# Branch rows split four to a step instead of two, and the branch projections dealt out from two steps sooner

## The chip, the cores and the metric

The kernel runs on one NeuronCore of a Trainium2 chip. The metric is the device time of one launch, in microseconds (us), as the median of several runs. TensorE (PE) does the matrix products; VectorE (DVE), ScalarE (ACT) and GpSimd (POOL) work on rows; SyncE (SP) issues most of the DMA transfers. Each engine takes its own instructions in program order and waits on semaphores for the others, so an instruction that waits holds up everything behind it on its engine.

## The reference, cut to what matters

One layer of a hybrid decoder for 1024 prompt tokens and 32 sample tokens. After a joint input projection three branches run (a state-space scan, dilated attention, attention into a memory); each is projected, gated, and the sum goes through an output projection.

```
h = RMSNorm(x);  u = h @ w_in
y_ssd = RMSNorm(ssd_scan(...) * silu(z))          # 16 heads x 64, chunks of 128 tokens
y_att = dilated_attention(...) * silu(z_att)
y_mem = memory_attention(...) * silu(z_mem)
merged = g0*(y_ssd @ w_br_ssd) + g1*(y_att @ w_br_att) + g2*(y_mem @ w_br_mem)
y = RMSNorm(x + merged @ w_out)
```

## The kernel before

**Precision by splitting.** A product in fp32 is made of three matmuls on a high part (fp32r) and a remainder: high x high, high x remainder, remainder x high (L2268 to L2270). So every operand is split first: ScalarE copies the value into the high part, VectorE subtracts that from the value and writes the remainder. For the weights that is L1363 and L1701, once for each chunk of 256 columns ("split" and "low" in the plan). A chunk's weights are loaded into one shared buffer, and its split is done two chunks ahead.

**Branch rows.** The attention and memory outputs lie in memory transposed, as eight rows of 128 partitions x 1056 tokens, 528 KB each: rows 0 to 3 of attention, 4 to 7 of memory. Before the branch projections each row is loaded by SyncE (L1110, "yal" in the plan) into one of three buffers in turn (yraw, acc1, acc0), copied by ScalarE into the high part (L1595) and subtracted by VectorE (L2094); the last two are "ya" in the plan. The load of row k waits until the remainder of row k-3 is made, since it takes that buffer. The eight rows of the scan's output are treated likewise ("yb": L1130, L1602, L2098), later.

**The scan.** The prompt runs in eight tiles of 128 tokens, here tiles 0 to 7 (tile 6 is the seventh), the sample tokens as a tile 8. The steps of tile c:

- step 0: TensorE transposes the tile (L2651 to L2656), ScalarE copies it out of PSUM (L1613 to L1616), VectorE weights it (L2150 to L2160). SyncE loads the tile (L1148), but only when the readout of the tile before is done.
- steps 1 and 2: decay matrices, two groups of four heads each: TensorE broadcasts (L2667), ScalarE takes a relu (L1628) and an exp (L1632), VectorE masks (L2167).
- step 3: products within the tile (L2687), then the readout of the state (L2695), which writes the PSUM banks 3 and 4. Before it, "step 6" of the tile before: TensorE transposes that tile's normed rows into the same banks (L2705), ScalarE copies them out (L1643) and GpSimd stores them (L1318). The readout waits for that copy, and the transposes wait for the relus of all four groups of the current tile.
- step 4: the tile's output and the new state on VectorE (L2188 to L2214); the second half of the state on TensorE (L2679) waits for VectorE's first half.
- step 5: square, root and norm of the output rows (L1635, L1637, L2219 to L2224).

**Order.** A function, plan(), writes one list of steps by hand; every engine walks through that list and issues its part of each step. Up to tile 6 step 0 the scan is mixed with the last input projections; entries 31 to 34 of the list "core" (tile 6, steps 1 to 4) carry the branch rows; the entries behind them are mixed, by the function spread(), with the branch projections ("p1"): 48 pieces of 12 matmuls (128 x 352, four rows deep), in four chunks (52 to 55) of two output tiles, three thirds of the tokens, and two branches. VectorE multiplies each piece by a gate (L2115, or L2117 and L2119 for the second branch); SyncE loads the gates (L1026, "p1g"), and GpSimd stores each finished output tile (L1290). A piece needs one of three PSUM banks, so TensorE runs at most three pieces ahead of VectorE. The first piece waits for all eight branch rows. Behind p1 come the projection of the scan's output ("p2", chunks 56 to 59, which wait for all eight yb rows) and the output projection.

The plan puts "low" of a chunk behind the next step 3 of a tile if that is within 15 places of its "split", and else directly behind the split.

Of the kernel before, what the change touches and what calls it, by code (L numbers as in the profile page):

```python
# [122 lines left out]
def plan():  # L123
# [73 lines left out]
    def spread(groups, steps):  # L197

        out, done = [], 0
        for i, g in enumerate(groups):  # L200
            out += g
            upto = len(steps) * (i + 1) // len(groups)
            for step in steps[done:upto]:
                out += step
            done = upto
        return out
# [54 lines left out]
    def gate_steps(k):  # L261

        steps = []
        for n in take(k):
            steps += [[s] for s in project(n) + [("split", n)]]
        return steps
# [26 lines left out]
    core = []  # L293
# [7 lines left out]
    core += [[(q, b)] for b in range(BS) for q in ("ssd_sb", "ssd_sd", "ssd_so")]  # L301
    core += [[("ssd_st",)], [("ssd_sy",)]]
    core += [[("ssd", NB, q)] for q in (4, 5, 6)] + [[], []] + [[("yb", k)] for k in range(KT8)]
    n_gate, n_ya = 31, 4
    core[n_gate - 3] += [("yal", k) for k in range(3)]
    for i in range(n_ya):
        core[n_gate + i] += [("yal", k) for k in ((3, 4), (5, 6), (7,), ())[i]]
        core[n_gate + i] += [("ya", 2 * i), ("ya", 2 * i + 1)]
    sched += spread(core[:n_gate], gate_steps(len(fill_src)))
    for x in core[n_gate:n_gate + n_ya]:  # L310
        sched += x
# [18 lines left out]
    for s in [s for s in sched if s[0] == "silu" and s[2] == 1]:  # L330
        i = sched.index(s)
        sched.insert(i + 3, sched.pop(i))
    for s in [s for s in sched if s[0] == "split" and ("low", s[1]) not in sched]:
        i = sched.index(s)
# [5 lines left out]

def build_program(nc, io, outs):
    chunks, sched, units, sets, values, part_end = plan()
    n_chunks = len(chunks)
    order = {}
# [2425 lines left out]
```

## Time and profile before

| | |
|---|---|
| median of 3 runs | 2211.18 us (2209.74 to 2226.33) |
| profiled execution, its own time | 2218.64 us |
| its span, first to last instruction | 2216.9 us |
| mean granted clock of TensorE | 0.959 of full |
| TensorE busy | 2048.2 us, 92% of the span |
| VectorE, ScalarE, GpSimd busy | 1056.7, 804.3 and 237.7 us |

The profile is of one execution, whose time lies 7.5 us above the median. The stretch that the change touches runs from about 1775 us (tile 6, step 1) to 1997 us (the first p2 piece), a tenth of the span.

### The profile page before, as it was taken

How to read it: one execution, taken by the hardware profiler on the slowest of the kernel's cores; microseconds unless marked ns; L12 is line 12 of the kernel's file. 1: busy time of each engine (PE TensorE's matmuls, PEld its weight loads, DVE VectorE, ACT ScalarE, POOL GpSimd, SP SyncE). 2: the span in 40 equal slices, each digit the busy share in tenths (PEclk: the TensorE clock that was granted, in tenths of full speed). 3: DMA queues.
4: the chain of work that ended last, by engine and by line, in shares of the span. 5: the costliest groups of instructions: out<-in, count | busy, mean ns of one | idle time of the engine just before them, and what ended most of it. 6: DMA issues, size and time to landing. Idle time of an engine off the chain costs nothing.

```text
span 2216.9 us, 35597 instructions
## 1 busy us (share of the span) xinstructions
PE 2048.2 (92%) x14571; PEld 1950.5 (88%) x14571; DVE 1056.7 (48%) x2058; ACT 804.3 (36%) x1730; POOL 237.7 (11%) x358
## 2 busy tenths in 40 slices
PE   5999998999989999999989889999999979979897
PEld 4899998999889999999989679768999968969897
DVE  5214665525453535353346862465444466454423
ACT  5223443223433333324634111554445463132202
POOL 1001121100001010112212000001111111100000
PEclk9999999999999999999999887999999989989998
DMA  6211241211111111112265664474242445554322
GB/s 207 87 59 41 80 121 60 75 46 50 37 39 56 56 51 57 63 65 83 72 201 182 210 199 140 163 249 152 87 134 77 168 138 172 175 185 134 132 83 102
DMA packets 166994, 248.77 MB, mean 112 GB/s; under 512 B 19701, under 2 KB 114613, under 8 KB 166805
## 3 DMA queue, kind: packets, MB, share of 16 engines
q1 hardware_dynamic: 144576, 179.51, 25.9%
q0 software_dynamic: 22256, 66.98, 8.5%
q8 instruction: 116, 1.90, 0.4%
q14 instruction: 46, 0.38, 0.1%
HBM read 179.74 MB, written 66.70 MB: 111 GB/s over the span
## 4 chain that ended last, share of the span: by engine, by line
PE 72%; DVE 9%; ACT 7%; DMA 6%; issue 5%; SPq 1%; DVEq 0%; POOL 0%; ACTq 0%; POOLq 0%
PE bank L2268 18%; PE bank L2269 17%; PE bank L2270 17%; PE bank L2464 2%; DVE w_lo L1701 2%; DMA acc<-acc_T 2%; PE bank L2439 2%; PE bank L2422 1%; PE bank L2687 1%; DMA w_raw<-in_w_in 1%; ACT soft L1502 1%; PE bank L2400 1%; ACT w_hi L1363 1%; DMA gate<-y_T 1%; ACT Lm L1628 1%
## 5 line engine op out<-in xcount | busy, mean ns | idle before, releaser
L2268 PE MATMUL bank<-w_hi,hT_hi 128*128 128x256 f32 (+1 forms) x1848 | 536.1, 290 | 12.4 <-ACT rows L1438 6.5
L2269 PE MATMUL bank<-w_lo,hT_hi 128*128 128x256 f32 (+1 forms) x1848 | 523.9, 283 | 0.0
L2270 PE MATMUL bank<-w_hi,hT_lo 128*128 128x256 f32 (+1 forms) x1848 | 523.2, 283 | 0.0
L2268 PE MATMUL bank<-hT_hi,w_hi 128*128 128x352 f32 x1344 | 456.7, 340 | 14.7 <-DVE w_lo L1701 8.1
L2270 PE MATMUL bank<-hT_hi,w_lo 128*128 128x352 f32 x1344 | 444.2, 330 | 0.0
L2269 PE MATMUL bank<-hT_lo,w_hi 128*128 128x352 f32 x1344 | 443.7, 330 | 0.0
L2268 PEld LDWEIGHTS bank<-w_hi,hT_hi 128*128 128x128 f32 (+1 forms) x1848 | 349.0, 189 | 14.5 <-issue 11.7
L2270 PEld LDWEIGHTS bank<-w_hi,hT_lo 128*128 128x128 f32 (+1 forms) x1848 | 350.0, 189 | 0.6
L2269 PEld LDWEIGHTS bank<-w_lo,hT_hi 128*128 128x128 f32 (+1 forms) x1848 | 349.0, 189 | 0.7
L2268 PEld LDWEIGHTS bank<-hT_hi,w_hi 128*128 128x128 f32 x1344 | 263.2, 196 | 18.1 <-DVE w_lo L1701 8.3
L2269 PEld LDWEIGHTS bank<-hT_lo,w_hi 128*128 128x128 f32 x1344 | 263.6, 196 | 1.4
L2270 PEld LDWEIGHTS bank<-hT_hi,w_lo 128*128 128x128 f32 x1344 | 261.3, 194 | 0.0
L1701 DVE TENSOR_TENSOR w_lo<-w_raw,w_hi 128x2048 fp32r<-128x2048 f32 x64 | 146.3, 2286 | 132.6 <-ACT w_hi L1363 132.6
L1438 ACT ACTIVATE rows<-bank 128x256 f32<-128x256 f32 (+2 forms) x172 | 64.7, 379 | 284.6 <-PE bank L2270 240.5
L1363 ACT ACTIVATE w_hi<-w_raw 128x2048 fp32r<-128x2048 f32 x64 | 121.9, 1905 | 109.4 <-PE bank L2270 55.4
L1472 ACT ACTIVATE fstage<-bank 128x256 f32<-128x256 f32 (+5 forms) x168 | 56.8, 454 | 250.7 <-PE bank L2270 250.6
L1502 ACT ACTIVATE soft<-soft,nmax 128x256 f32<-128x256 f32 (+1 forms) x224 | 100.0, 448 | 75.8 <-DVE nmax L1872 75.5
L1775 DVE TENSOR_TENSOR small<-rows,con 128x32 f32<-128x32 f32 (+1 forms) x108 | 20.6, 190 | 187.6 <-ACT rows L1438 187.2
L1852 DVE TENSOR_TENSOR soft<-bank,con 128x256 f32<-128x256 f32 (+1 forms) x96 | 47.7, 537 | 51.3 <-PE bank L2422 51.3
L2464 PE MATMUL bank<-V,softT 128*128 128x64 f32 x560 | 67.8, 270 | 0.8 <-issue 0.8
L2464 PEld LDWEIGHTS bank<-V,softT 128*128 128x128 f32 x560 | 66.6, 192 | 1.0 <-issue 1.0
L1901 DVE COPY obuf<-bank 128x256 f32<-128x256 f32 x48 | 20.2, 421 | 99.1 <-PE bank L2464 99.1
(437 smaller groups left out, 3164.6 us busy)
## 6 DMA issues: line engine op xcount, KB each, us to landing
w_raw<-in_w_in SPq DMA_DIRECT2D x96, 512.0 KB, 4.7
kvring<-in_cache_win_kv SPq DMA_DIRECT2D x144, 256.0 KB, 3.5
feat_T<-fstage POOLq DMA_DIRECT2D x40, 528.0 KB, 3.5
fstage<-feat_T SPq DMA_DIRECT2D x16, 528.0 KB, 4.4
kvring<-in_cache_mem_kv SPq DMA_DIRECT2D x32, 256.0 KB, 3.4
xc<-feat_T SPq DMA_DIRECT2D x8, 1024.0 KB, 5.3
o_rows<-obuf POOLq DMA_DIRECT2D x48, 132.0 KB, 2.0
mo<-o_rows SPq DMA_DIRECT2D x24, 264.0 KB, 4.0
```

The costliest lines, as they stand in the source:

```text
L1363: act.activation(w_hi[:, n % 2, :, :], w_raw[:, :, :], ACT.Copy).then_inc(s_whi, 1)
L1438: act.activation(dst, psum, func).then_inc(s_pjev, 1)
L1472: ins = act.activation(dst[:, to], psum[:, c0:c1], func)
L1502: ins = act.activation(soft[:, a % 2, h, 0:w], soft[:, a % 2, h, 0:w], ACT.Exp, bias=nmax[:, a % 2, h:h + 1], scale=scale, accum_out=total)
L1628: ins = act.activation(l[:, h, :], D_of(c, qq)[:, h, :], ACT.Relu, scale=-1.0, bias=sc[0:m, 2, SH * c + 4 * qq + h:SH * c + 4 * qq + h + 1])
L1701: dve.tensor_tensor(w_lo[:, n % 2, :, :], w_raw[:, :, :], w_hi[:, n % 2, :, :].bitcast(F32), ALU.subtract).then_inc(s_wlo, 1)
L1852: ins = dve.tensor_tensor(dst, src, con[:, c0:c0 + w].unsqueeze(1).broadcast_to([P, 2, w]), ALU.add)
L2268: pe.matmul(out, xh(k), wh(k), start=(k == 0), stop=False)
L2269: pe.matmul(out, xh(k), wl(k), start=False, stop=False)
L2270: ins = pe.matmul(out, xl(k), wh(k), start=False, stop=(k == nk - 1))
L2439: ins = pe.transpose(bank[5 + h // 2][:, c0:c0 + P], soft[:, a % 2, h, P * k:P * k + P], ident)
L2464: ins = pe.matmul(bank[7][:, HD * h:HD * h + HD], softT[:, a % 2, h, k, :], V[:, b0 + k, c0:c0 + HD], start=(k == 0), stop=(k == kb - 1))
```

## The change

Entries 31 and 32 of "core" now carry four branch rows each, where entries 31 to 34 carried two each; the loads move along. The branch projections are mixed in from entry 33 on (tile 6, step 3) instead of entry 35.

```diff
-    n_gate, n_ya = 31, 4
+    n_gate, n_ya = 31, 2
     core[n_gate - 3] += [("yal", k) for k in range(3)]
     for i in range(n_ya):
-        core[n_gate + i] += [("yal", k) for k in ((3, 4), (5, 6), (7,), ())[i]]
-        core[n_gate + i] += [("ya", 2 * i), ("ya", 2 * i + 1)]
+        core[n_gate + i] += [("yal", k) for k in ((3, 4, 5, 6), (7,))[i]]
+        core[n_gate + i] += [("ya", 4 * i + k) for k in range(4)]
     sched += spread(core[:n_gate], gate_steps(len(fill_src)))
     for x in core[n_gate:n_gate + n_ya]:
         sched += x
```

No instruction is added or removed. ScalarE in tile 6, before (L1628 and L1632 are the decay groups, L1595 the branch rows, L1643 the copy of tile 5's output):

```order
L1632 ACTIVATE Lm<-Lm 128x512
L1595 ACTIVATE hT_hi<-yraw 128x1056
L1595 ACTIVATE hT_hi<-acc 128x1056
L1628 ACTIVATE Lm<-bank,sc 128x128 x4
L1632 ACTIVATE Lm<-Lm 128x512
L1628 ACTIVATE Lm<-bank,sc 128x128 x4
L1632 ACTIVATE Lm<-Lm 128x512
L1595 ACTIVATE hT_hi<-acc 128x1056
L1595 ACTIVATE hT_hi<-yraw 128x1056
L1643 ACTIVATE yst<-bank 128x512 x2
L1595 ACTIVATE hT_hi<-acc 128x1056 x2
```

The same place now:

```order
L1632 ACTIVATE Lm<-Lm 128x512
L1595 ACTIVATE hT_hi<-yraw 128x1056
L1595 ACTIVATE hT_hi<-acc 128x1056 x2
L1595 ACTIVATE hT_hi<-yraw 128x1056
L1628 ACTIVATE Lm<-bank,sc 128x128 x4
L1632 ACTIVATE Lm<-Lm 128x512
L1628 ACTIVATE Lm<-bank,sc 128x128 x4
L1632 ACTIVATE Lm<-Lm 128x512
L1595 ACTIVATE hT_hi<-acc 128x1056 x2
L1595 ACTIVATE hT_hi<-yraw 128x1056
L1595 ACTIVATE hT_hi<-acc 128x1056
L1643 ACTIVATE yst<-bank 128x512 x2
```

The copies of rows 2 and 3 moved ahead of the two decay groups of step 2, and those of rows 4 to 7 all ahead of the copy of tile 5's output. VectorE in the sample tile (tile 8, steps 4 and 5; L1701 is the remainder of the weights of chunk 56), before:

```order
L2117 TENSOR_TENSOR fstage<-bank,fstage 128x352
L2119 TENSOR_TENSOR acc<-acc,fstage 128x352
L2188 TENSOR_TENSOR yo<-bank,sc 32x512 x2
L2197 TENSOR_TENSOR yy<-yy,yo 32x1024
L2210 TENSOR_TENSOR yy<-yy,skip 32x1024
L2214 TENSOR_TENSOR yy<-yy,zt 32x1024
L1701 TENSOR_TENSOR w_lo<-w_raw,w_hi 128x2048
L2219 TENSOR_SCALAR small<-small 32x1
```

The same place now:

```order
L2117 TENSOR_TENSOR fstage<-bank,fstage 128x352
L2119 TENSOR_TENSOR acc<-acc,fstage 128x352
L1701 TENSOR_TENSOR w_lo<-w_raw,w_hi 128x2048
L2188 TENSOR_TENSOR yo<-bank,sc 32x512 x2
L2197 TENSOR_TENSOR yy<-yy,yo 32x1024
L2210 TENSOR_TENSOR yy<-yy,skip 32x1024
L2214 TENSOR_TENSOR yy<-yy,zt 32x1024
L2115 TENSOR_TENSOR acc<-bank,fstage 128x352
```

The weight remainder moved from behind the sample tile's output to ahead of it. SyncE's loads of the scan's rows (L1130), with the last gate load (L1026) between them, as a piece of the difference:

```order
 L1026 DMA fstage<-feat_T 128x1056 x2
 L1130 DMA yraw<-y_T 128x1056
 L1130 DMA gate<-y_T 128x1056
+L1026 DMA fstage<-feat_T 128x1056
 L1130 DMA acc<-y_T 128x1056
-L1026 DMA fstage<-feat_T 128x1056
 L1130 DMA yraw<-y_T 128x1056
 L1130 DMA gate<-y_T 128x1056
```

The gate load moved from behind the third of these rows to ahead of it.

## Rows read from the trace of the kernel before

**Rows 1.** Windows: length, then busy us of each engine, granted clock, DMA.

```profile
1808.00:1840.00 32.00, 24.54 (x153) 22.84 (x152) 17.59 (x28) 13.10 (x29) 2.83 (x2) 0.89 0.22 62
1840.00:1950.00 110.00, 109.34 (x797) 104.85 (x797) 55.44 (x131) 26.46 (x51) 14.67 (x16) 0.97 0.56 184
```

**Rows 2.** Timeline of ScalarE in tile 6: start, us, what, idle before.

```profile
1784.94 1.12 ACT L1628 ACTIVATE Lm<-bank,sc 128x128 f32<-128x128 f32 x4
...
1788.33 1.07 ACT L1595 ACTIVATE hT_hi<-acc 128x1056 fp32r<-128x1056 f32 x1
1789.30 1.07 ACT L1595 ACTIVATE hT_hi<-yraw 128x1056 fp32r<-128x1056 f32 x1
1790.27 1.06 ACT L1643 ACTIVATE yst<-bank 128x512 f32<-128x512 f32 x2
```

**Rows 3.** Timeline of VectorE in tile 6.

```profile
1781.43 0.69 DVE L2167 TENSOR_TENSOR Lm<-Lm,CBm 128x512 f32<-128x512 f32 x1 [4.08 <-ACT Lm L1632]
...
1784.10 1.26 DVE L2094 TENSOR_TENSOR hT_lo<-yraw,hT_hi 128x1056 fp32r<-128x1056 f32 x1 [0.28 <-ACT hT_hi L1595]
```

**Rows 4.** Timeline of SyncE's queue in tile 6: the load of row 3.

```profile
1785.38 0.34 SPq L1110 DMA_DIRECT2D yraw<-y_T  x1
```

**Rows 5.** DMA issues from 1785 to 1786 us: size, us to landing.

```profile
yraw<-y_T SPq DMA_DIRECT2D x1, 528.0 KB, 3.4
```

**Rows 6.** Source view of L1110, all eight loads of branch rows.

```profile
DMA to landing us min/median/max: 3.3/6.3/7.9
```

**Rows 7.** Timeline of TensorE from 1786 to 1812 us.

```profile
1787.90 1.94 PE L2705 MATMUL bank<-con,yy 128*128 128x128 f32 x8 [3.35 <-ACT Lm L1628]
...
1795.06 1.95 PE L2695 MATMUL bank<-state,xc 128*128 128x256 f32 x8
1800.30 1.13 PE L2679 MATMUL bank<-xdec,btok 128*128 128x256 f32 x4 [3.30 <-DVE state L2203]
1802.43 1.97 PE L2651 MATMUL bank<-con,xc 128*128 128x128 f32 x8 [1.00 <-DMA xc<-feat_T]
...
1806.24 0.40 PE L2268 MATMUL bank<-hT_hi,w_hi 128*128 128x352 f32 x1
```

**Rows 8.** Timeline of all engines from 1935 us: the sample tile's end.

```profile
1945.79 1.03 PE L2742 MATMUL bank<-con,yoT 128*32 128x128 f32 x8
...
1948.86 1.92 ACT L1363 ACTIVATE w_hi<-w_raw 128x2048 fp32r<-128x2048 f32 x1 [4.50 <-PE bank L2270]
...
1949.92 1.28 DVE L2188 TENSOR_TENSOR yo<-bank,sc 32x512 f32<-32x512 f32 x2
...
1954.96 2.29 DVE L1701 TENSOR_TENSOR w_lo<-w_raw,w_hi 128x2048 fp32r<-128x2048 f32 x1
...
1959.09 1.06 PE L2705 MATMUL bank<-con,yy 32*128 32x32 f32 x8 [8.40 <-DVE yy L2224]
```

**Rows 9.** Chain that ended last, 1940 to 2012 us: start, us, what.

```profile
1947.47 0.16 PE bank L2269
...
1963.38 0.29 PE bank L2269
...
1966.82 0.54 DVE acc L2115
...
1978.96 7.73 DMA gate<-y_T
...
1989.11 5.13 DMA gate<-y_T
```

**Rows 10.** Timeline of SyncE's queue at the scan's rows.

```profile
1967.89 0.32 SPq L1130 DMA_DIRECT2D yraw<-y_T  x1
...
1978.12 0.32 SPq L1026 DMA_DIRECT2D fstage<-feat_T  x1
```

**Rows 11.** DMA issues from 1955 to 1975 us.

```profile
yraw<-y_T SPq DMA_DIRECT2D x1, 528.0 KB, 4.2
...
y_T<-yst POOLq DMA_DIRECT2D x1, 128.0 KB, 4.2
```

**Rows 12.** Timeline of TensorE: the first p2 piece.

```profile
1996.74 0.63 PE L2268 MATMUL bank<-y_s_hi,w_hi 128*128 128x352 f32 x1 [2.47 <-issue]
```

## The prediction

> **What bounds the kernel now.** I read the busy shares of the page first (in the table above), then windows over the touched stretch, then the timelines of single engines where TensorE stands still. TensorE is busy for 92% of the span, so a change of order pays only in the few places where TensorE waits, and costs where it makes a new wait. From 1840 to 1950 us there is nothing to win: TensorE is busy for 109.34 of 110 us [rows 1]. A delay that reaches 1840 is therefore not made good before 1950. The waits lie on either side. In tile 6 TensorE waits 3.35 us for ScalarE's relus, 3.30 us for VectorE's state and 1.00 us for the load of tile 7 [rows 7]; in tile 7, from 1808 to 1840, it is busy for 24.54 of 32 us [rows 1]; and at the end of the sample tile it waits 8.40 us for the normed rows [rows 8]. From there to the first p2 piece at 1996.74 [rows 12] the chain that ended last runs through the loads of the scan's rows [rows 9], so the time of p2's start decides the end, and all behind it is unchanged.
>
> **Part 1, tile 6: the rows.** Before, ScalarE does two row copies, then the two decay groups of step 2 from 1784.94, then row 3 at 1789.30 without a wait, then tile 5's output at 1790.27 [rows 2]. Now four row copies stand ahead of the groups. Row 3 takes the buffer of row 0, so its load goes out only when row 0's remainder is made, at 1784.10 + 1.26 = 1785.36 [rows 3]; SyncE did issue it at 1785.38 [rows 4], and it took 3.4 us [rows 5], so it lands at 1788.8. Until now the decay groups covered that. With the groups behind it ScalarE stands until 1788.8, copies for 1.0 us, and the first relu starts at 1789.8 instead of 1784.94: 4.9 us late. TensorE's transposes at 1787.90 wait for these relus [rows 7], so they start at about 1792.8.
>
> The second wait is worse to see. The readout, at 1795.06 [rows 7], needs the copy of tile 5's output out of banks 3 and 4, and that copy now stands behind rows 4 to 7. Row 7 takes row 4's buffer. Row 4's copy starts where ScalarE is done with the groups, 1788.33 + 4.9 = 1793.2 [rows 2], its remainder is made 1.07 + 1.26 us later, at 1795.6, and only then row 7's load goes out. The eight loads took 3.3 to 7.9 us, 6.3 in the middle [rows 6]. I take 3.4 us, as for row 3 [rows 5], because by then little else is in the queues: the store of tile 5's output itself now comes later. That gives 1799.0; row 7's copy of 1.07 and the output's copy of 1.06 us [rows 2] make it 1801.2. The readout starts 6.1 us late; with the ends 3.3 and 6.4 us for the load, 6.0 to 9.1 late.
>
> The Trainium skill ("DMA: Bandwidth & Descriptors", section "Rules for kernel authors") speaks against this change: issue a transfer early, compute, and wait for it late. Row 3 shows both sides: its 3.4 us cost nothing behind two decay groups. By that page's cost of a transfer, 2.0 us and the bytes at 436 GB/s, a row of 528 KB is an estimated 3.2 us, and the sum below would be 0.2 us less.
>
> **Part 2, tile 6: the first projection piece.** From the readout to the second half of the state it is 1800.30 - 1795.06 = 5.24 us [rows 7], so that half starts at 1806.4 and ends at 1807.5. Now the first piece stands here, ahead of tile 7's transposes. All eight remainders are made by then (row 7's copy ends at 1800.1, 1.26 us for the remainder), so the piece runs at once. A piece of 12 matmuls, 0.16 us each at the full clock and 0.29 after an idle stretch [rows 9], takes 2.0 to 3.5 us; TensorE has just waited, and I take 2.6: 1810.1. It covers the load of tile 7, which goes out at the end of the readout: before at 1795.06 + 1.95 = 1797.0, to land at 1802.43 [rows 7]; now at 1803.2, to land at 1808.6. Tile 7's transposes took 1806.24 - 1802.43 = 3.8 us with the clock low; behind a running piece I take 2.3 and get 1812.4. That is 6.2 us after 1806.24, with one piece of 2.0 us already done. "Two steps sooner" is thus one piece of 48 moved past one tile boundary. From there each piece stands where its predecessor stood, one place earlier against the scan, and I price that at nothing: the work per slot differs by one 0.5-us operation on VectorE, which is busy for 17.59 of the 32 us to 1840 and for 55.44 of the next 110 [rows 1]. Without that cover it would be 0.5 us at a few places.
>
> Chunk 53's weight remainder moves too, to directly behind its split, ahead of the decay masks. VectorE was idle for 4.08 us there [rows 3] while the remainder takes 2.29 [rows 8]: nothing.
>
> **Part 3, the sample tile's end.** With one piece less to do, the last piece of chunk 54, whose end starts the weight copy at 1948.86 [rows 8], ends at 1948.8 + 6.2 - 2.0 - 0.9 = 1952.1 (the 0.9 are the sample readout's transposes L2742, from 1945.79 to the next matmul [rows 8], which now come behind it). The weights of chunk 56 follow: ScalarE's copy starts when that piece is done and takes 1.92 us, VectorE's remainder 2.29 us [rows 8]. Before, the remainder lay behind the tile's output, under the square; now the output waits for it, until 1952.1 + 0.1 + 1.9 + 2.3 = 1956.4. The output then takes 1954.96 - 1949.92 = 5.0 us, and the norm to TensorE's transposes 1959.09 - 1954.96 = 4.1 us [rows 8]: 1965.6, which is 6.5 us late. So the earlier piece is spent again: VectorE's chain, not TensorE, sets this point, and TensorE waits for about as long as before.
>
> **Part 4, the scan's rows.** Before, SyncE held the first row's load until 1967.89, behind a gate load that needs VectorE's product of 1966.82 [rows 9, 10]: 8.8 us after the transposes. That piece is now the first behind the transposes and not the second, so the gate load goes out some 5.3 us after them (transposes 1.06 [rows 8], a piece of up to 3.5, 0.2 for the handing over, the product 0.54 [rows 9]), and the store of the sample tile (4.2 us to landing [rows 11], issued 1.9 us after the transposes) becomes the later one: 6.5 us, a gain of 2.3. Against that, the last gate load, which went out at 1978.12 [rows 10], now holds the third row. It needs the second branch's product, which stands behind the first row on VectorE: 6.5 + 4.2 (load [rows 11]) + 1.1 + 1.3 (split) + 1.1 = 14.2 us after the transposes, so the third row goes out at 14.5 and no longer together with the first two. The second batch of three (third to fifth row) I price as the second batch before, 6.3 to 8.5 us with 7.73 for its middle one [rows 9]: the fifth is split at 26.9 us, the eighth's load takes 5.1 more [rows 9] and its split 2.4: 34.4 us. Before it was 1996.7 - 1959.1 = 37.6. Gain 3.2 us; 1.5 if the third row's load is slowed by the gate load beside it, 4.5 if the smaller first batch lands sooner.
>
> **Sum.** + 6.5 - 3.2 = + 3.3 us, ends + 1.3 (earliest load, a piece at the full clock, best tail) and + 9 (late load, slow piece, poor tail). The profiled execution of 2218.64 us would become 2222; the median lies 7.5 us lower, so 2214.5 us. A measurement of this kernel can tell about 1% (22 us) from no change, so this is no change that one can tell.
>
> **Rivals.**
>
> *The head's delay is swallowed in tile 7.* TensorE waits there for 7.5 us of 32 [rows 1]. If those waits hung on something that does not move with tile 7's transposes, the 6.2 us would vanish, and the tail's gain alone would stay: 2211.2 - 3.2 = 2208.0. Against it: that stretch hardly loads anything (DMA share 0.22 [rows 1]), so the waits are ScalarE's and VectorE's own chain behind the transposes, which moves along. Chance 0.13.
>
> *The loads bunch.* Rows 4 to 7 are asked for more closely, and the third scan row shares the queues with a gate load. If row 7 took 7.9 us [rows 6] (4.5 more than I took) and the tail gained nothing, that would be 6.5 + 4.5 = 11 us: 2222, slower. It decides from a landing of row 7 above about 6 us. For it: half of the eight loads took 6.3 or more. Against it: those went out in threes or beside a tile's store. Chance 0.14.
>
> *The clock stays low through tile 7.* TensorE now stands still for 3.35 + 4.9 = 8.2 us in one piece ahead of the transposes, where it stood 3.35 before [rows 7]. If the granted clock, 0.89 from 1808 to 1840 [rows 1], were half there throughout, 24.5 busy us would become up to 24.5 x 0.89 / 0.5 = 43.6: 19 us more, 2234 in all, slower by 1%. Against it: after the 8.40 us at 1959 the matmuls were back at the full rate within some 6.5 us. The Trainium skill ("TensorE: Matmul & The Clock Gate", section "What's actually happening") has the low level as the default that activity lifts; by that, too, it comes back once pieces run again. Chance 0.03.
>
> **How the numbers follow.** The forecast has 0.70. The range, 2207 to 2222, holds its ends (2212.5 to 2220), the first rival and the second's edge; what is left out is the clock and what I have not seen. Faster by over 1% would take nearly all waits of the touched stretch at once (3.35 + 3.30 + 1.00 + 7.5 + 8.40 = 23.6 us): 0.01. Slower by over 1%: the clock, and a little: 0.04. The rest, 0.95, within 1%.
>
> **What would show it.** In the changed kernel's timelines: ScalarE idle for about 3 us before row 3's copy and for 2 us or more before row 7's; TensorE's transposes of tile 5 near 1793 and its readout near 1801, waiting for L1643; the first piece ahead of tile 7's transposes; the weight remainder ahead of L2188 in the sample tile; TensorE's transposes of tile 8 near 1966; the first p2 piece near 2000. Wrong would be: no wait before the readout (a faster load or another buffer than I read), or a busy stretch to 1950 that is not simply shifted.

## The result, and the profile after

| | before | after |
|---|---|---|
| median, 19 runs each | 2214.68 us | 2223.68 us |
| ratio after / before, 95% interval | | 1.0036, 1.0020 to 1.0052 |
| profiled execution, its own time | 2218.64 us | 2228.25 us |
| its span | 2216.9 us | 2226.5 us |
| TensorE busy | 2048.2 us | 2050.0 us |

The change costs 8.0 us (4.4 to 11.5, from the ratio; the medians differ by 9.0). One run after, of 6436.59 us, is left out of the ratio. The forecast was 3.3, with ends 1.3 and 9, on a base of 2211.2, the median of three runs; with 19 runs the kernel before stands at 2214.7. So of the 9.2 us between 2214.5 and 2223.7, 3.5 are the base and 5.7 the sum (4.7 by the ratio). The time lies 1.7 us above the range's end of 2222. That the cost lies within the ends of the sum is luck: it is made of other parts than the sum, as the table of shifts shows. TensorE's busy time is nearly the same: the loss is mostly waiting. The stretch that the change touches goes from the last decay group of tile 6 to the first p2 piece; one window each (columns as in [rows 1]). Before:

```profile
1782.48:1996.74 214.26, 181.02 (x1185) 171.29 (x1185) 121.21 (x212) 71.21 (x123) 24.26 (x24) 0.90 0.52 170
```

After:

```profile
1781.62:2007.70 226.08, 183.79 (x1185) 174.68 (x1185) 120.32 (x212) 71.30 (x123) 24.77 (x25) 0.88 0.49 163
```

The stretch is 11.8 us longer in these two profiles, more than the 8.0 us of all runs. TensorE waits for 42.3 us of it instead of 33.2, and works for 2.8 us longer on the same 1185 matmul records: that is the clock, 0.88 instead of 0.90.

**Tile 6.** Timeline of TensorE before, the rows that were not shown ahead:

```profile
1782.48 2.07 PE L2667 MATMUL bank<-con,sc 128*128 128x128 f32 x8 [1.82 <-ACT Lm L1628]
...
1791.34 3.88 PE L2687 MATMUL bank<-xdt,Lm 128*128 128x64 f32 x32
...
1808.25 1.95 PE L2667 MATMUL bank<-con,sc 128*128 128x128 f32 x16
```

TensorE after, in answer to [rows 7] and [rows 12], with the sample tile:

```profile
1781.62 2.08 PE L2667 MATMUL bank<-con,sc 128*128 128x128 f32 x8 [1.81 <-ACT Lm L1628]
1791.71 1.94 PE L2705 MATMUL bank<-con,yy 128*128 128x128 f32 x8 [8.01 <-ACT Lm L1628]
...
1795.15 6.93 PE L2687 MATMUL bank<-xdt,Lm 128*128 128x64 f32 x32
1801.87 3.29 PE L2695 MATMUL bank<-state,xc 128*128 128x256 f32 x8
1808.46 2.07 PE L2679 MATMUL bank<-xdec,btok 128*128 128x256 f32 x4 [3.30 <-DVE state L2203]
1809.97 0.85 PE L2268 MATMUL bank<-hT_hi,w_hi 128*128 128x352 f32 x1
...
1812.75 1.04 PE L2651 MATMUL bank<-con,xc 128*128 128x128 f32 x8
...
1816.86 1.95 PE L2667 MATMUL bank<-con,sc 128*128 128x128 f32 x16
...
1866.00 1.94 PE L2687 MATMUL bank<-xdt,Lm 32*32 32x64 f32 x32 [0.23 <-DVE Lm L2167]
1869.46 1.94 PE L2723 MATMUL bank<-con,xc 128*128 128x128 f32 x8 [1.52 <-DVE yy L2172]
1871.05 0.64 PE L2268 MATMUL bank<-hT_hi,w_hi 128*128 128x352 f32 x1
...
1873.97 2.05 PE L2731 MATMUL bank<-Lm,xdec 32*128 32x128 f32 x16
...
1925.14 2.02 PE L2731 MATMUL bank<-xc,xdec 32*128 32x128 f32 x16 [1.69 <-DVE Lm L2235]
...
1972.93 1.06 PE L2705 MATMUL bank<-con,yy 32*128 32x32 f32 x8 [8.72 <-DVE yy L2224]
...
2007.70 0.63 PE L2268 MATMUL bank<-y_s_hi,w_hi 128*128 128x352 f32 x1 [6.14 <-issue]
```

ScalarE after, in answer to [rows 2]:

```profile
1787.76 1.08 ACT L1595 ACTIVATE hT_hi<-yraw 128x1056 fp32r<-128x1056 f32 x1 [2.61 <-DMA yraw<-y_T]
1788.75 1.12 ACT L1628 ACTIVATE Lm<-bank,sc 128x128 f32<-128x128 f32 x4
...
1797.73 1.08 ACT L1595 ACTIVATE hT_hi<-acc 128x1056 fp32r<-128x1056 f32 x1 [2.06 <-DMA acc<-y_T]
1798.72 1.07 ACT L1643 ACTIVATE yst<-bank 128x512 f32<-128x512 f32 x2
```

ScalarE stands 2.61 us for row 3 and 2.06 us for row 7, as foretold. The readout, however, shows no wait: the products ahead of it (L2687) took 6.93 us instead of 3.88, at a granted clock of 0.50, the lower level (1.2 GHz), and ended later than ScalarE's copy at 1799.8.

**The sample tile.** TensorE before, between the tile's products and its first state product:

```profile
1855.76 1.94 PE L2687 MATMUL bank<-xdt,Lm 32*32 32x64 f32 x32 [0.22 <-DVE Lm L2167]
1857.63 0.43 PE L2268 MATMUL bank<-hT_hi,w_hi 128*128 128x352 f32 x1
...
1859.65 1.04 PE L2723 MATMUL bank<-con,xc 128*128 128x128 f32 x8
1860.62 2.05 PE L2731 MATMUL bank<-Lm,xdec 32*128 32x128 f32 x16
```

Before, a projection piece (1857.63) stood between the products and L2723, and TensorE did not wait. Now the piece comes after L2723, and ahead of L2723 TensorE waits 1.52 us for VectorE's copy. It waits 1.69 us more at 1925, and there it is not a piece that is missing. ScalarE and VectorE after, ahead of that wait:

```profile
1918.23 1.92 ACT L1363 ACTIVATE w_hi<-w_raw 128x2048 fp32r<-128x2048 f32 x1 [4.26 <-DMA w_raw<-in_w_br_mem]
...
1920.25 2.29 DVE L1701 TENSOR_TENSOR w_lo<-w_raw,w_hi 128x2048 fp32r<-128x2048 f32 x1 [7.21 <-ACT w_hi L1363]
```

ScalarE's split of the next weights waited for their load, VectorE's remainder came behind the split and ahead of VectorE's L2235, and TensorE waited for L2235.

**The scan's rows.** SyncE's queue after, in answer to [rows 10]:

```profile
1978.91 0.32 SPq L1130 DMA_DIRECT2D yraw<-y_T  x1
...
1986.43 0.32 SPq L1026 DMA_DIRECT2D fstage<-feat_T  x1
1986.79 0.43 SPq L1130 DMA_DIRECT2D acc<-y_T  x1
```

The first row goes out 6.0 us behind the transposes (8.8 before), the third 13.9 us, behind the gate load.

The forecast's steps against the two traces, as shifts counted from tile 6's last decay group (1782.48 before, 1781.62 after, so 0.86 is added to each difference):

| start of | before | after | shift foretold | shift |
|---|---|---|---|---|
| tile 5's transposes, L2705 | 1787.90 | 1791.71 | 4.9 | 4.7 |
| tile 6's readout, L2695 | 1795.06 | 1801.87 | 6.1 | 7.7 |
| second half of the state, L2679 | 1800.30 | 1808.46 | 6.1 | 9.0 |
| tile 7's first decay group, L2667 | 1808.25 | 1816.86 | 6.2 | 9.5 |
| sample tile's products, L2687 | 1855.76 | 1866.00 | 6.2 | 11.1 |
| its state product, L2731 | 1860.62 | 1873.97 | 6.2 | 14.2 |
| its last transposes, L2705 | 1959.09 | 1972.93 | 6.5 | 14.7 |
| first p2 piece | 1996.74 | 2007.70 | 3.3 | 11.8 |

### The profile page after: what moved, and what is told of

The parts are those of the page before. It is cut to its first block, busy times and chain, and to the rows that moved or that the text cites. A ratio compares the mean times of both kernels' runs of the same rounds, so it can differ in the third digit from the quotient of the medians.

```text
span 2226.5 us, 35596 instructions
## 1 busy us (share of the span) xinstructions
PE 2050.0 (92%) x14571; PEld 1953.1 (88%) x14571; DVE 1057.7 (48%) x2058; ACT 804.6 (36%) x1730; POOL 237.5 (11%) x358
## 4 chain that ended last, share of the span: by engine, by line
PE 75%; DVE 9%; ACT 6%; issue 5%; DMA 4%; SPq 1%; DVEq 0%; POOL 0%; ACTq 0%; POOLq 0%
PE bank L2268 19%; PE bank L2269 18%; PE bank L2270 18%; PE bank L2464 2%; DVE w_lo L1701 2%; PE bank L2439 2%; PE bank L2687 1%; PE bank L2422 1%; DMA w_raw<-in_w_in 1%; ACT w_hi L1363 1%; ACT soft L1502 1%; PE bank L2400 1%; DVE softT L1960 1%; PE bank L2679 1%; PE bank L2667 1%
## 5 line engine op out<-in xcount | busy, mean ns | idle before, releaser
L2268 PE MATMUL bank<-w_hi,hT_hi 128*128 128x256 f32 (+1 forms) x1848 | 537.0, 291 | 10.9 <-ACT rows L1438 6.4
L1701 DVE TENSOR_TENSOR w_lo<-w_raw,w_hi 128x2048 fp32r<-128x2048 f32 x64 | 146.3, 2286 | 139.6 <-ACT w_hi L1363 139.5
L2268 PE MATMUL bank<-y_s_hi,w_hi 128*128 128x352 f32 x192 | 63.1, 329 | 6.1 <-issue 6.1
```

Of the source, the lines that this page charges most:

```text
L1701: dve.tensor_tensor(w_lo[:, n % 2, :, :], w_raw[:, :, :], w_hi[:, n % 2, :, :].bitcast(F32), ALU.subtract).then_inc(s_wlo, 1)
L2268: pe.matmul(out, xh(k), wh(k), start=(k == 0), stop=False)
```

## The experiments

"Longer" is what the stretch from tile 6's last decay group to the first p2 piece has over the 214.3 us of the kernel before; "wait" is TensorE's waiting in it (its length less the busy time, 33.2 us in the kernel before); "tail" is the time from the sample tile's last transposes to the first p2 piece (37.65 us before). The matmuls that e12 and e13 add count as work. These three come from one profile each; the time is the ratio's, against the kernel before on the same chip.

| run | edit | against before, us (95%) | longer | wait | tail |
|---|---|---|---|---|---|
| after |  | +8.0 (4.4 to 11.5) | +11.8 | 42.3 | 34.8 |
| e1 | rows alone | +9.5 (6.2 to 12.6) | +3.7 | 39.2 | 36.3 |
| e2 | dealing alone | +9.5 (5.8 to 13.5) | +8.2 | 40.5 | 34.4 |
| e3 | output's copy ahead of rows 4 to 7 | +10.6 (5.5 to 15.7) | +5.9 | 43.1 | 34.4 |
| e4 | one split a place later | +14.4 (10.0 to 18.8) | +10.7 | 44.1 | 34.4 |
| e5 | both splits back | +5.5 (0.9 to 10.2) | +5.0 | 37.7 | 34.4 |
| e6 | rows three and five | +8.8 (4.4 to 13.5) | +9.6 | 44.3 | 34.9 |
| e7 | e5 and e6 | +6.6 (2.4 to 10.8) | +7.5 | 41.3 | 35.7 |
| e8 | before, scan rows direct | -3.5 (-7.3 to 0.4) | -3.2 | 28.5 | 30.8 |
| e9 | after, branch rows direct | +10.0 (6.2 to 13.9) | +8.7 | 37.7 | 34.4 |
| e10 | before, unchanged | +2.4 (-1.3 to 6.0) | -0.5 | 31.9 | 37.0 |
| e11 | after, all mended | 0.0 (-4.2 to 4.4) | -0.3 | 33.5 | 30.1 |
| e12 | after, TensorE kept busy | +7.3 (3.5 to 10.8) | +8.1 | 39.0 | 34.4 |
| e13 | before, TensorE kept busy | +2.0 (-1.5 to 5.8) | +2.3 | 32.2 | 36.7 |
| e14 | before, scan rows direct, copies early | -7.5 (-11.7 to -3.5) | -8.7 | 27.7 | 28.1 |

In eleven of the fifteen rows the profile's stretch and the time agree within 3 us; in the changed kernel, e1, e3 and e4 they differ by 3.7 to 5.8 us, so one profile places a loss but doesn't measure it to better than that.

Theory A: the loss is TensorE's waiting, in tile 6 by the rows and in the sample tile by the shifted projections. Theory B, first rival: only one of the two parts matters. Theory C, later: the low clock behind the longer wait is a cost of its own.

**e1, the rows alone.**

```diff
-    for x in core[n_gate:n_gate + n_ya]:
+    for x in core[n_gate:n_gate + 4]:
...
-    sched += spread(core[n_gate + n_ya:], steps)
+    sched += spread(core[n_gate + 4:], steps)
```

> The rows four to a step as in the changed kernel, but the projections dealt from entry 35, as before the change. Theory A (the rows make the loss in tile 6: TensorE first waits for the rows' copies, then runs tile 6's products and readout at the lower clock level): tile 5's transposes start 4.6 us later than before the change, the readout 7.6 and the second half of the state 9.0 us later; tile 7's transposes then wait for their load again, 9 us late, and nothing behind gives it back, the sample tile included, where the gap of 1.5 us ahead of L2723 should be gone: 2222 to 2225 us, 8 to 10 above the kernel before. Theory B (the rows' waits are absorbed and the shifted projections make the loss): within 2 us of the kernel before.

Up to the sample tile this is as Theory A says: transposes 4.8 us late, readout 6.5, state 7.6, tile 7's decay groups 9.2, and no wait ahead of the sample tile's L2723. The time is as it says too. But "nothing behind gives it back" is wrong in this profile: the sample tile's L2731 is 8.2 us late and its last transposes only 5.1, since the same matmuls between them were busy for 86.9 us instead of 90.1, at a granted 0.97 instead of 0.95. Here the products ran faster, and the readout shows the wait for ScalarE that they had covered in the changed kernel (2.06 us, for L1643).

**e2, the dealing alone.** The row steps are those of the kernel before, with 2 in place of `n_ya` in the same two lines.

> The rows two to a step as before the change, but the projections dealt from entry 33, as in the changed kernel. Theory A: tile 6 is as before up to the second half of the state; the first piece waits ahead of tile 7's transposes for row 7's remainder until 1806 us, which costs 2 to 3 us there; the sample tile loses another 3 us where the weights' split and no piece stands behind L2687 (TensorE waits 1.5 us ahead of L2723 and runs the next piece at the low level), and the scan's rows give 3 back: 2 to 4 us above the kernel before, about 2218. Theory B: it carries the whole loss, 8 to 9 us, 2223.

Tile 6 is as before up to the state, and the sample tile loses what it loses in the changed kernel (1.51 and 1.43 us of waiting). But the price was missed, 9.5 us against 2 to 4: the first piece, now ahead of tile 7's transposes, waits 4.88 us and then runs at the low level, since row 7's copy comes late. ScalarE there:

```profile
1799.59 1.08 ACT L1595 ACTIVATE hT_hi<-acc 128x1056 fp32r<-128x1056 f32 x1 [4.31 <-DMA acc<-y_T]
```

With the rows as before, the early piece waits for them; with the rows early, the readout does. By the times each part alone costs as much as both, within intervals of some 3.5 us to either side; by the stretches the two add up (3.7 and 8.2 against 11.8). Which of these holds is open, but neither part is free, and Theory B falls.

**e3, the order on ScalarE.** Rows 4 to 7 move to the next step, behind the copy of tile 5's output.

```diff
-        core[n_gate + i] += [("ya", 4 * i + k) for k in range(4)]
+        core[n_gate + 2 * i] += [("ya", 4 * i + k) for k in range(4)]
```

> The changed kernel with the copies of rows 4 to 7 behind the copy of tile 5's output on ScalarE (L1643) instead of ahead of it. If the readout is set by TensorE's own products at the lower clock level, as the profile of the changed kernel suggests (no wait ahead of the readout), it starts where it did, 10.2 us behind the transposes of tile 5, and the time is that of the changed kernel within 1 us. If the readout waits for that copy, as the prediction had it, it starts 2 to 3 us sooner and the time falls by as much.

The readout starts 4.3 us late, with no wait, 3.4 us sooner than in the changed kernel. It still comes right behind its products, and those ran faster here (3.51 us to the readout instead of 6.72, at a granted 0.79 from the transposes on), so the run does not tell the copy from the clock. And the time shows no gain: the remainders of these rows now stand on VectorE ahead of tile 6's state, and TensorE waits 6.27 us for that instead of 3.30.

```profile
1810.10 2.07 PE L2679 MATMUL bank<-xdec,btok 128*128 128x256 f32 x4 [6.27 <-DVE state L2203]
```

**e6, three rows and five.**

```diff
-        core[n_gate + i] += [("ya", 4 * i + k) for k in range(4)]
+        core[n_gate + i] += [("ya", k) for k in ((0, 1, 2), (3, 4, 5, 6, 7))[i]]
```

> The changed kernel with three rows in tile 6 step 1 and five in step 2, so that row 3's copy, which waits for its load, stands behind the two decay groups again and rows 3 to 7 stand ahead of the copy of tile 5's output. Theory A (the loss in tile 6 is the order on ScalarE against the loads): tile 5's transposes start 1.0 us later than before the change instead of 4.7, the readout 3 to 4 us later instead of 6.5 to 7.7, and tile 7's decay groups about 4 us later with one piece done: 2218 to 2219 us, 5 less than the changed kernel. Theory B (row 7's load or the clock sets it, whatever stands ahead): the readout is still 6 us or more late, and the time stays near 2223.

Theory B of that run holds. The transposes are only 1.0 us late, but the readout then waits 6.06 us for L1643, which stands behind rows 4 and 7:

```profile
1790.00 1.08 ACT L1595 ACTIVATE hT_hi<-acc 128x1056 fp32r<-128x1056 f32 x1 [3.50 <-DMA acc<-y_T]
...
1795.77 1.08 ACT L1595 ACTIVATE hT_hi<-acc 128x1056 fp32r<-128x1056 f32 x1 [2.15 <-DMA acc<-y_T]
1796.76 1.06 ACT L1643 ACTIVATE yst<-bank 128x512 f32<-128x512 f32 x2
```

The wait only moves along. Wherever row 7 is asked for late and stands ahead of that copy (the changed kernel, e1, e4 to e7 and e12), the readout is 6.5 to 7.7 us late.

**e9, no buffers in turn.** The branch rows are loaded straight into the tile of their remainders, when the last input projection is done; ScalarE copies from there and VectorE subtracts in place.

```diff
...
-                    sp.dma_start(ya_slot(k), yT[8 + k]).then_inc(s_kv[k % 3], 16)
+                    sp.dma_start(yAl[:, k, :].bitcast(F32), yT[8 + k]).then_inc((s_kv + s_eld)[k], 16)
...
-                    act.activation(yAh[:, k, :], ya_slot(k), ACT.Copy).then_inc(s_yah, 1)
+                    act.activation(yAh[:, k, :], yAl[:, k, :].bitcast(F32), ACT.Copy).then_inc(s_yah, 1)
```

> The changed kernel with the eight branch rows loaded straight into the tile that takes their remainders (hT_lo), all eight issued when the last input projection is done, instead of through three buffers in turn; rows, steps and dealing as in the changed kernel. Theory A (what the rows cost in tile 6 is the turn of the three buffers: rows 3 and 7 are asked for only when rows 0 and 4 are made): ScalarE waits for no row any more; tile 5's transposes start 2 us later than before the change (two copies more ahead of the groups) and not 4.7, the readout about 2 us later and not 6.5 to 7.7, tile 7's decay groups 1 to 2 us later with one piece done; 6 to 7 us less than the changed kernel, about 2216. Theory B (the four copies in a row on ScalarE and VectorE, not the loads, or the clock, make the loss): the readout is still 5 us or more late, and the time within 2 us of the changed kernel's.

ScalarE's waits are gone, and the transposes are 1.9 us late, as Theory A says. But the readout is 4.9 us late and the time no better. TensorE:

```profile
1787.65 1.94 PE L2705 MATMUL bank<-con,yy 128*128 128x128 f32 x8 [5.29 <-ACT Lm L1628]
...
1791.09 6.93 PE L2687 MATMUL bank<-xdt,Lm 128*128 128x64 f32 x32
1797.81 2.97 PE L2695 MATMUL bank<-state,xc 128*128 128x256 f32 x8
```

With nothing for the readout to wait for, the products ran at the low level throughout (granted 0.50) and took the place of the wait. That raised Theory C.

**e12 and e13, TensorE kept busy.** Behind tile 6's last decay group, matmuls of 128x256 into a bank that nobody reads: 36 in the changed kernel, 16 in the kernel before.

```diff
-                            ins.then_inc(s_dD, 1)
+                            ins.then_inc(s_dD, 1); [... pe.matmul(bank[n_act_proj % 3][:, 0:CW], w_hi[:, 0, 0, 0:P], w_hi[:, 0, 1, :], start=True, stop=True) for i in range(37 * ((c, qq) == (6, 3)))]
```

> The changed kernel with 36 matmuls of 128x256 more, behind the last decay group of tile 6 (L2667), into a PSUM bank that nobody reads; 0.1 us each at the full clock and 0.2 at the low one, so that TensorE works for 4 to 7.7 us of the 8.0 us that it stands still there. Theory C (a part of the loss is the low clock that follows TensorE's long wait): tile 5's transposes start where they did, but from them to tile 7's decay groups it takes 18 to 20 us instead of 25.1, since products, readout, first piece and tile 7's transposes run at the full clock: about 2218 us, 5 to 6 less than the changed kernel. Theory D (the low level there comes and goes by itself, or follows something else): the stretch stays between 23 and 25 us, and the time within 2 us of the changed kernel's.

> The kernel before with 16 such matmuls at the same place, where it waits 3.35 us. Theory C: the granted clock from tile 5's transposes to the readout is above 0.9 instead of 0.5 to 0.73, and that stretch takes 5.7 us instead of 7.2 to 10.2: 2 to 4 us less than the kernel before. Theory D: no difference.

e12, TensorE:

```profile
1788.24 6.40 PE L2668 MATMUL bank<-w_hi 128*128 128x256 f32 x36
1796.76 1.06 PE L2705 MATMUL bank<-con,yy 128*128 128x128 f32 x8 [2.12 <-ACT Lm L1628]
...
1798.52 3.68 PE L2687 MATMUL bank<-xdt,Lm 128*128 128x64 f32 x32
1805.79 3.46 PE L2695 MATMUL bank<-state,xc 128*128 128x256 f32 x8 [3.59 <-ACT yst L1643]
```

Theory C is right on the level and wrong on its price; by the price Theory D holds (24.4 us from the transposes to tile 7's decay groups, 25.1 in the changed kernel). The clock did come back during the added work: the products took 3.68 us, at a granted 1.00. But then the readout waited 3.59 us for ScalarE and was 6.7 us late all the same, tile 7's decay groups 8.9 instead of 9.5. In e13 the readout came 1.7 us sooner, and the state's second half then waited 6.66 us for VectorE instead of 3.30. Its time is 2.0 us above the kernel before (-1.5 to 5.8) and not 2 to 4 below. The low level and the waits lie beside each other: taking one away shows the other.

**e4, e5 and e7, the empty places.** The list that is dealt out holds 52 places: 48 pieces and four splits of weights, which give TensorE nothing to do. In e4 the first split changes places with the piece and gate load behind it; in e5 the first two splits do, with the gate load staying behind the split; e7 is e5 with e6's rows.

```diff
-    sched += spread(core[n_gate + n_ya:], steps)
+    sched += spread(core[n_gate + n_ya:], steps[:12] + [steps[13], steps[12]] + steps[14:])
```

```diff
+    for i in (12, 25): steps[i], steps[i + 1] = steps[i + 1][:1], steps[i] + steps[i + 1][1:]
     sched += spread(core[n_gate + n_ya:], steps)
```

> The changed kernel with the weights' split of chunk 52 one place later among the projection pieces, so that a piece and not the split stands behind L2687 of the sample tile. If the empty place makes the loss there, TensorE's wait ahead of L2723 (1.52 us) is gone, the piece behind it runs at the full rate, and the stretch from L2687 to L2731 takes 4.9 us with its piece, as before the change, instead of 8.0: 3 us less than the changed kernel, 2220 to 2221. If the wait has another cause, it stays and the time with it.

> The changed kernel with the weights' splits of chunks 52 and 53, places among the projection pieces that hold no matmul, moved back to the slots of the sample tile that they had before the change (one piece later), the gate loads staying behind them. Theory: in the changed kernel these two empty places fall into slots where TensorE needs a piece as cover, behind L2687 (wait 1.52 us ahead of L2723) and behind the fifth sample sequence's L2723 (wait 1.69 us ahead of L2731); moved back, both waits are gone, and from tile 7's norm to the sample readout the changed kernel loses 3 to 4.5 us less: about 2220 us. Rival: the gaps come from the whole sequence being one place early, not from the empty places; then they stay, and the time too.

> Both edits together: rows three and five to a step, and the two empty places back in their slots. If the two losses are independent and make up what the change cost, this is 8 us below the changed kernel, 2214 to 2216, no different from the kernel before. If they are not the causes, it stays above 2220.

In all three profiles the 1.52 us ahead of L2723 are gone, and from L2687 to L2731 it takes 4.9 us again instead of 8.0. e5, TensorE:

```profile
1860.87 1.94 PE L2687 MATMUL bank<-xdt,Lm 32*32 32x64 f32 x32 [0.23 <-DVE Lm L2167]
1862.74 0.43 PE L2268 MATMUL bank<-hT_hi,w_hi 128*128 128x352 f32 x1
...
1864.77 1.04 PE L2723 MATMUL bank<-con,xc 128*128 128x128 f32 x8
```

In e5 the later 1.69 us are gone too, and the last transposes are 8.2 us late instead of 14.7; 1.6 us of that difference are the clock, since the same matmuls behind L2731 were busy for 87.0 us instead of 88.6. Its time is 2.5 us below the changed kernel's; the intervals overlap, so the time alone doesn't show it.

The traces do. All six profiles with the splits where the changed kernel has them (itself, e2, e3, e6, e9, e12) have the first wait, at 1.51 or 1.52 us; none of the three with both splits back (e5, e7, e11) and none of the six with the old dealing has either wait. The second follows the load of the weights: ScalarE waited for it 4.26, 4.07, 4.01, 3.35, 3.02 and 2.84 us, and TensorE then 1.69, 1.50, 1.43, 0.77, 0.44 and 0.31, each time 2.5 to 2.6 us less; e4, whose second split stays, has 3.61 and 1.04. At its first split e4 closed the gap and opened a larger one by the same chain: with the gate load ahead, the weights were asked for later, ScalarE's split of them waited 4.54 us for the load, VectorE's remainder for the split, and TensorE 3.72 us for VectorE:

```profile
1871.45 3.20 PE L2731 MATMUL bank<-xc,xdec 32*128 32x128 f32 x16 [3.72 <-DVE Lm L2235]
```

e7 fails like e6: its readout waits 5.00 us, and at 6.6 us above the kernel before the two edits together do not give the loss back.

**e10, the kernel before again.**

> The kernel before, unchanged, as a control of what the time and a single profile can tell. If the low level of TensorE's clock follows the waits alone, its second profile shows tile 6 as the first did: 7.2 us from tile 5's transposes to the readout, granted clock 0.73. If it comes and goes from run to run, that stretch differs by up to 3 us with the same waits. The ratio of times should be 1.000 within 0.002.

Its second profile shows 7.25 us and 0.72 for tile 5's transposes to the readout (7.16 and 0.73 at first). That would fit a level that follows the waits. But from the readout to tile 7's decay groups it took 14.85 us at 0.77, where the first took 13.19 at 0.87; and e8, whose order is the same up to the sample tile, took 10.16 us at 0.50 there, with the same 3.34 us of waiting ahead.

**e8, e11 and e14, the tail.** The scan's rows are loaded straight into y_s_lo, the tile of their remainders, as the branch rows in e9. e8 issues all eight behind the sample tile's last transposes; e11 is the changed kernel with e5's and e9's edits and the rows issued four and four around a gate load; e14 is the kernel before with the rows so issued, and their copies dealt out ahead of the last gate's sigmoid. The loads in e11 and e14 (e8 has all eight in one loop), then the list of e14:

```diff
...
-                    sp.dma_start(yb_slot(k), yT[k]).then_inc(s_kv[k % 3], 16)
+                    for k in range(4 * s[1], 4 * s[1] + 4):
+                        sp.dma_start(yBl[:, k, :].bitcast(F32), yT[k]).then_inc((s_kv + s_eld)[k], 16)
```

```diff
-    core += [[("ssd", NB, q)] for q in (4, 5, 6)] + [[], []] + [[("yb", k)] for k in range(KT8)]
+    core += [[("ssd", NB, q)] for q in (4, 5)] + [[("ssd", NB, 6), ("ybl", 0)], [], [], [("ybl", 1), ("yb", 0)]] + [[("yb", k) for k in g] for g in ((1, 2), (3,), (4,), (5,), (6, 7), (), ())]
```

> The kernel before, with the eight rows of the scan's output loaded straight into the tile that takes their remainders (y_s_lo), all eight issued behind the sample tile's last transposes and ahead of the gate loads, copied from there by ScalarE and subtracted in place by VectorE, instead of through three buffers in turn. It tests the reading that the chain of buffers and gate loads sets the start of p2. If so, the eighth row lands 19 to 20 us behind the transposes, its remainder is made at 22, and p2 starts when the remaining p1 pieces are done, 25 to 28 us behind the transposes instead of 37.7: 2202 to 2205 us, 9 to 12 below the kernel before. If the loads only bunch, or the p1 pieces wait for their gates behind them, p2 starts at 34 or later, and the gain is 3 us or less.

> The changed kernel with its three losses mended and its gain extended: branch rows loaded straight into hT_lo, the two empty places back in their slots, and the scan's rows loaded straight into y_s_lo, four ahead of the next to last gate load and four behind it. If the three places are independent, tile 6 costs 2 us, the sample tile nothing, and p2 starts 27 to 30 us behind the sample tile's last transposes instead of 37.7: 2204 to 2207 us, faster than both kernels. If the gate loads or the remaining pieces set p2's start, it stays at 34 us behind the transposes, and the time is 2211 to 2213.

> The kernel before with the scan's rows loaded straight into y_s_lo, four ahead of the next to last gate load and four behind it, and their copies all ahead of the sigmoid of the last gate, which in the earlier run held ScalarE for 5 to 7 us with rows already landed. If rows and gates in ScalarE's order set the start of p2, it starts 25 to 28 us behind the sample tile's last transposes instead of 37.7 and 30.8: 2205 to 2208 us. If the queues are full, the last gate still lands 8 us or more after its issue and p2 starts at 30: 2210.

e8's tail is 30.8 us and not 25 to 28: its last two gate loads went out behind eight rows and took 9.9 us (median), and ScalarE stood 7.5 us for the first of them with rows already landed. e11 has that gate between the rows, but the last gate then holds ScalarE for 5.5 us. Its tail is 30.1 us, its sample tile loses nothing, but tile 7's decay groups are 7.9 us late and not 2, as in e9; so it equals the kernel before and misses the forecast. e14 gets the copies past the gate: tail 28.1 us, the time 2204.86 us, 7.5 us below the kernel before (ratio 0.9966, 0.9947 to 0.9984) and by the two ratios some 15 below the changed one. TensorE in e14:

```profile
1954.74 1.06 PE L2705 MATMUL bank<-con,yy 32*128 32x32 f32 x8 [8.41 <-DVE yy L2224]
...
1982.80 0.40 PE L2268 MATMUL bank<-y_s_hi,w_hi 128*128 128x352 f32 x1 [3.26 <-DVE fstage L2117]
```

## Why the prediction missed, point by point

In the two traces the stretch is 11.8 us longer and not 3.3. Of the 8.5 us between, 3.3 arose in tile 6, 1.6 in tile 7, 3.1 between the sample tile's products and its first state product, and 0.5 behind it. Both signs that the prediction named as wrong came up: no wait before the readout, and a stretch to 1950 that is not simply shifted.

*Tile 5's transposes, 4.9 us late: right* (4.7), by row 3's load, which ScalarE now waits for.

*The readout, 6.1 us late by row 7's load: the mechanism right, the size nearly.* Row 7 landed 3.2 us after its issue at 1794.52 (3.4 taken). ScalarE's copy of the output ended at 1799.8, which alone would make it 5.6 us. e1, e4, e6, e7 and e12 show the readout waiting for that copy and 6.5 to 6.8 us late; in the changed kernel TensorE's own slow products covered the wait and ended 1.6 us later than foretold.

*"From the readout to the second half of the state it is 5.24 us": mis-sized.* It took 6.59. The readout ran mostly at the low level (granted 0.59), 3.29 us instead of 1.95. In all, tile 6 cost 9.5 us against 6.2. The term left out the clock after the wait that the prediction itself foretold. The rival that had the low level through tile 7, at 19 us, had the right place and the wrong length: the level came back within the first piece, which took 2.78 us (2.6 taken) and covered tile 7's load as foretold.

*"From there each piece stands where its predecessor stood, one place earlier against the scan, and I price that at nothing": the step that failed.* The places are not alike. Four of 52 hold a split and no matmul. One place earlier, the first fell where TensorE had used a piece as cover, and L2687 to L2731 took 3.1 us longer: 1.52 us of waiting, then L2723 and half of the next piece at the low level. The second brought VectorE's remainder of 2.29 us, late behind the weights' load, ahead of work that TensorE needs: 1.69 us. e5, e7 and e11 show it: put back, both waits are gone. The reason given was that the work per slot differs by one 0.5-us operation on VectorE; what a slot gives TensorE, and that a split's remainder moves too, was left out.

*The same price of nothing in tile 7: 1.6 us.* From tile 7's first decay group to the sample tile's products TensorE waited 8.6 us instead of 8.1 and was busy for 40.5 instead of 39.4 on the same 278 matmul records; the piece at 1824.68 ran for ten of its matmuls at the low level and took 3.35 us instead of 2.0. The ten profiles with the new dealing wait 8.5 to 9.6 us there, the six with the old one 7.0 to 8.2, so the waiting goes with the dealing. How it arises is open.

*"A delay that reaches 1840 is therefore not made good before 1950": not so.* TensorE's being busy throughout does not fix the length: its clock varied, and e1 made 3.1 us good.

*The sample tile's end: right.* The wait of 8.72 us (8.40 before) is there, with the weights' remainder ahead of the output, and the delay grows by 0.5 us (0.3 foretold). VectorE:

```profile
1961.60 2.29 DVE L1701 TENSOR_TENSOR w_lo<-w_raw,w_hi 128x2048 fp32r<-128x2048 f32 x1 [0.99 <-ACT w_hi L1363]
1963.81 1.27 DVE L2188 TENSOR_TENSOR yo<-bank,sc 32x512 f32<-32x512 f32 x2
```

*The tail, 3.2 us gained: right.* 34.8 us against 37.65, a gain of 2.9, with the rows issued 6.0 and 13.9 us behind the transposes (6.5 and 14.5 foretold). All runs that keep the new dealing and the old loads of the scan's rows have 34.4 to 35.7, all with the old dealing and the old loads 36.3 to 37.65.

*The rivals.* The head's delay was not swallowed in tile 7 (9.5 us at its start, 10.9 at its readout). The loads did not bunch: row 7 took 3.2 us.

*"No change that one can tell": wrong.* With 19 runs of each kernel the interval of the ratio, 1.0020 to 1.0052, leaves out 1.

What stays open: the low level in tile 6 was there in full in five of the profiles (the changed kernel, e5, e8, e9, e11), one of them with the order of the kernel before, so how much of its cost is the change's is not settled; e12 bounds it, since with the clock back up tile 7's decay groups came 0.6 us sooner and the time fell by 0.7 us only, inside both intervals. e9's profile has 4.5 us of added waiting and 4.2 of added busy time on the same matmuls, which is the clock: L2687 to L2731 of the sample tile took 9.5 us (8.0 in the changed kernel, with the same wait), at a clock of 0.57, and one profile cannot say whether that is usual. And no run gives the loss of tile 6 back: every edit there moved the wait.

## What to carry to other kernels

Where work is dealt out evenly from a list, look for the places in the list that give the bounding engine nothing: moved by one, they land in other slots, and a slot that was covered no longer is. Look as well at what such a place gives the other engines (here a load, a split and a remainder). Before removing a wait, ask what lies beside it: here a row's load, VectorE's remainders and TensorE's own slow products each stood ready to take the readout's wait, and only the tail, where nothing stood behind, paid. With buffers in turn a load waits until the row before it in its buffer is used up; a load straight into the tile that the result overwrites needs no buffer; it paid here in the tail, most where no late gate load stood ahead of the copies (e14), and not in tile 6 (e9).

## What the runs showed of the hardware

From tile 5's transposes to tile 6's readout the same instructions behind the same 3.3 us of waiting took 7.16 to 7.31 us in four profiles (granted clock 0.71 to 0.73) and, in e8, 10.16 us (0.50). Behind 8.0 to 8.2 us of waiting TensorE was busy with them for 6.60 us (e3, 0.79), 6.81 (e1), 7.74 (e4) and 10.16 (the changed kernel and e5, 0.50). So the length of the wait did not settle how long the low level lasted. The Trainium skill ("TensorE: Matmul & The Clock Gate", section "What's actually happening") calls the number of matmuls at the low level, at the start of one kernel, run-variable; these traces agree, in the middle of a kernel. So a single profile can be off by 3 us in such a place. TensorE's waits compare better between profiles: the first one in the sample tile reads 1.51 or 1.52 us in all six.

A stretch that TensorE fills has no fixed length either: the same 621 or 622 matmul records between the sample tile's L2731 and its last transposes were busy for 86.9 to 90.2 us in the sixteen profiles (granted 0.94 to 0.98).

Loads of 528 KB issued close together landed one after the other: ScalarE in e14 got its first four rows, issued within 1.8 us, 1.32 us apart (1964.04, 1965.36, 1966.69, 1968.01), which is some 410 GB/s, while the two gate loads of the same size behind eight rows in e8 took 9.9 us (median), and row 7, asked for alone in the changed kernel, 3.2.
